# Layer 0's carried-state convolution taps on GpSimd, paced over the input stage and three heads

## What is computed

```python
q, k, v, g_ret, ca, cb, ga, gb = split(rms_norm(x) @ w_in)
o, r_new = retention(q, k, v, r0)          # 4 heads; r0: carried state, 8 sequences x 4 heads x 256 x 512
y_ret = (silu(g_ret) * layer_norm(o)) @ w_ret_out
u = ca * sigmoid(cb)
padded = concatenate([c0, u])              # c0: the last 30 rows of u, carried, for each sample sequence
z = depthwise_conv(padded, conv_w) + conv_b   # 31 taps a channel
x = x + rms_norm((sigmoid(ga) * y_ret + sigmoid(gb) * conv_branch(z)) @ w_o)
x = x + rms_norm(swiglu_ffn(rms_norm(x)))
```

## Time and profile before

| what | value |
| --- | --- |
| median of three executions | 1622.85 us (1619.75 to 1623.2) |
| the profiled execution, its own time | 1627.17 us |
| its span, first to last instruction | 1625.4 us |
| TensorE busy | 1559.7 us, 96% of the span |
| VectorE busy | 1133.8 us, 70% |
| ScalarE busy | 666.1 us, 41% |
| GpSimd busy | 285.8 us, 18% |
| DMA | 275.69 MB, 170 GB/s on average |
| mean granted TensorE clock | 0.989 of full speed |

### The profile page before, as it was taken

The page is one execution under the profiler, slowest core; times in us unless marked ns, Lnnn a source line. Parts: engine busy times, 40 slices in busy tenths (PEclk is TensorE's granted clock), DMA queues, the critical chain, the costliest instruction groups (busy, mean ns, idle before and its releaser), DMA issues.

```text
span 1625.4 us, 28225 instructions
## 1 busy us (share of the span) xinstructions
PE 1559.7 (96%) x10008; PEld 1433.0 (88%) x10008; DVE 1133.8 (70%) x1684; ACT 666.1 (41%) x973; POOL 285.8 (18%) x257
## 2 busy tenths in 40 slices
PE   6988999999999999999989999999999999999997
PEld 5987878786899999999979979687779998999997
DVE  6999887887767577654456988779786675555544
ACT  4323434353455353433343335253445544444433
POOL 6971100001110019910000400001020100000000
PEclk8999999999999999999999999999999999999999
DMA  6444846556344424444435555647364442444443
GB/s 258 143 170 143 292 149 241 194 209 238 124 143 149 171 92 155 153 144 156 156 116 165 199 185 219 220 170 281 136 219 156 149 137 79 160 151 143 154 156 114
DMA packets 64562, 275.69 MB, mean 170 GB/s; under 512 B 7232, under 2 KB 7232, under 8 KB 55232
## 3 DMA queue, kind: packets, MB, share of 16 engines
q1 hardware_dynamic: 52560, 192.17, 34.7%
q0 software_dynamic: 11888, 82.04, 14.0%
HBM read 230.30 MB, written 43.89 MB: 169 GB/s over the span
## 4 chain that ended last, share of the span: by engine, by line
PE 77%; DVE 10%; issue 6%; DMA 4%; ACT 2%; DVEq 0%; POOL 0%; ACTq 0%
PE bank L414 22%; PE bank L416 21%; PE bank L415 21%; DMA rs_out<-state 3%; DVE wlo L1032 2%; DVE acc L1067 2%; PE bank L551 2%; DMA state<-r_in 2%; PE bank L448 1%; PE bank L586 1%; PE bank L568 1%; DVE state L1098 1%; PE bank L534 1%; PE bank L503 1%; DVE x L1336 1%
## 5 line engine op out<-in xcount | busy, mean ns | idle before, releaser
L414 PE MATMUL bank<-hhi,whi 128*128 128x320 f32 x2016 | 656.7, 326 | 11.8 <-DVE wlo L1032 9.2
L1032 DVE TENSOR_TENSOR wlo<-wring,whi 128x1024 fp32r<-128x1024 f32 x363 | 475.0, 1312 | 257.0 <-ACT whi L769 203.0
L416 PE MATMUL bank<-hhi,wlo 128*128 128x320 f32 x2016 | 624.8, 310 | 0.0
L415 PE MATMUL bank<-hlo,whi 128*128 128x320 f32 x2016 | 624.5, 310 | 0.0
L414 PEld LDWEIGHTS bank<-hhi,whi 128*128 128x128 f32 x2016 | 380.1, 189 | 73.1 <-issue 58.3
L415 PEld LDWEIGHTS bank<-hlo,whi 128*128 128x128 f32 x2016 | 380.7, 189 | 6.5 <-issue 3.8
L416 PEld LDWEIGHTS bank<-hhi,wlo 128*128 128x128 f32 x2016 | 380.1, 189 | 0.0
L769 ACT ACTIVATE whi<-wring 128x1024 fp32r<-128x1024 f32 x264 | 277.5, 1055 | 236.9 <-PE bank L416 236.5
L1067 DVE SCALAR_TENSOR_TENSOR acc<-up,par,acc 128x256 f32<-128x256 f32 x480 | 230.0, 544 | 0.0
L795 ACT ACTIVATE whi<-wring 128x1024 fp32r<-128x1024 f32 x96 | 101.4, 1056 | 99.6 <-PE bank L416 99.6
L799 ACT ACTIVATE sig<-bank 128x320 f32<-128x320 f32 x92 | 40.3, 438 | 209.0 <-PE bank L416 195.5
(11 more groups left out here) (155 smaller groups left out, 2012.2 us busy)
## 6 DMA issues: line engine op xcount, KB each, us to landing
wring<-w SPq DMA_DIRECT2D x364, 512.0 KB, 3.3
state<-r_in POOLq DMA_DIRECT2D x32, 1024.0 KB, 7.0
rs_out<-state POOLq DMA_DIRECT2D x32, 1024.0 KB, 5.4
rp_out<-pst POOLq DMA_DIRECT2D x8, 512.0 KB, 7.6
us<-c_in POOLq DMA_DIRECT2D x2, 1216.0 KB, 5.8
cs_out<-us POOLq DMA_DIRECT2D x2, 1216.0 KB, 8.2
cp_out<-up POOLq DMA_DIRECT2D x2, 1144.0 KB, 4.6
con<-consts POOLq DMA_DIRECT2D x1, 1420.0 KB, 9.7
```

What stands on the lines that cost most here:

```text
L414: pe.matmul(bank[g][:, 0:T], whi[j][:, k, :], hi, start=start and k == 0, stop=False)
L415: pe.matmul(bank[g][:, 0:T], whi[j][:, k, :], lo, start=False, stop=False)
L416: mm = pe.matmul(bank[g][:, 0:T], wlo[j][:, k, :], hi, start=False, stop=stop and k == n - 1)
L1032: return dve.tensor_tensor(dst, value, hi.bitcast(F32), ALU.subtract)
```

## The change

The carried taps of layer 0 are split up. Taps 0 to 3 start as before. Taps 4 to 17 each wait for `unit_done` to reach 2k - 6, so that they run one for every two units, the last of them behind unit 28, the end of head 0. The other twelve, taps 18 to 29, go into GpSimd's work on heads 0 and 1: one behind each of `store(0)`, `store(1)`, `rp_out`, `store(2)`, `store(3)` and the last load. The bias and the save `cs_out` follow behind head 1, and the 8 newest taps are put between the stores and loads of head 2: three behind `load_after(1)`, two behind `rp_out`, one behind `store(2)`, two behind `store(3)`. `cp_out` is issued behind tap 17. Layer 1's order stays, and so do the other engines' programs.

```diff
@@ past_taps becomes past_tap and past_bias; layer0_taps and new_tap are new
-            def past_taps(l, past, ptap, bias, weights):
+            def past_tap(l, past, ptap, weights, k):
...
+                n = min(DS, PAD - k)
...
+                pool.tensor_tensor(window(ptap if k else past, 0, n), window(us, k, n), tap, ALU.mult).then_inc(sample_conv_step, 1)
+                if k:
+                    pool.wait_ge(sample_conv_step, l * SAMPLE_OPS + 2 * k)
+                    pool.tensor_tensor(window(past, 0, n), window(past, 0, n), window(ptap, 0, n), ALU.add).then_inc(sample_conv_step, 1)
+
+            def past_bias(l, past, bias):
...
+            first_taps = iter(range(PAD))
+
+            def layer0_taps(n, unit=None):
+
+                for k in itertools.islice(first_taps, n):
+                    if unit is not None and k > 3:
+
+                        pool.wait_ge(unit_done, 2 * k - 6)
+                    past_tap(0, past0, stap, par[:, G_CW:NPAR], k)
+
+            def new_tap(l, i):
...
@@ in head(l, hd, last)
-                for q in range(2):
-                    store(q)
-                    load_after(q)
+                spread = l == 0 and hd < 2
+                newest = iter(range(DS) if l == 0 and hd == 2 else ())
+                store(0)
+                if spread:
+                    layer0_taps(1)
+                load_after(0)
+                store(1)
+                if spread:
+                    layer0_taps(1)
+                load_after(1)
+                if l == 0 and hd == 2:
+
+                    pool.wait_ge(u_saved, 32)
+                    for i in itertools.islice(newest, 3):
+                        new_tap(l, i)
 
                 pool.wait_ge(act_aux, H * AUX_ACT + 7)
                 pool.dma_start(rp_out[H], pst[:, :, :]).then_inc(pst_stored, 16)
+                if spread:
+                    layer0_taps(1)
+                for i in itertools.islice(newest, 2):
+                    new_tap(l, i)
                 store(2)
+                if spread:
+                    layer0_taps(1)
+                for i in itertools.islice(newest, 1):
+                    new_tap(l, i)
                 store(3)
+                for i in newest:
+                    new_tap(l, i)
                 if not last:
+                    if spread:
+                        layer0_taps(1)
                     load_after(2)
                     load_after(3)
+                if spread:
+                    layer0_taps(1)
@@ in the layer loop
-                    past_taps(0, past0, stap, par[:, G_CB:G_CW], par[:, G_CW:NPAR])
+                    layer0_taps(PAD - 12, U_CIN)
 
                 pool.wait_ge(u_ready, l * 16 + 16)
                 pool.dma_start(cp_out[l], up[:, :, :]).then_inc(u_saved, 16)
+                if l == 0:
+                    for hd in range(2):
+                        head(l, hd, False)
+                    past_bias(0, past0, par[:, G_CB:G_CW])
                 pool.wait_ge(sample_conv_step, l * SAMPLE_OPS + PAST_OPS)
                 pool.dma_start(cs_out[l], us[:, :, :, :]).then_inc(u_saved, 16)
-
-                pool.wait_ge(u_saved, l * 32 + 32)
-                new_taps(l)
-                for hd in range(HEADS - 1):
-                    head(l, hd, False)
+                if l > 0:
+
+                    pool.wait_ge(u_saved, l * 32 + 32)
+                    for i in range(DS):
+                        new_tap(l, i)
+                    for hd in range(2):
+                        head(l, hd, False)
+                head(l, 2, False)
                 conv_pair_sum(l, 1)
                 head(l, HEADS - 1, True)
```

More of the change, by code:

```diff
@@ L385, in _ @@
                     pool.wait_ge(ffn_step, l * (2 * FT) + 2 * FFN_FIRST)
-                    past_taps(l + 1, past, ptap, cw[:, 0:KT], cw[:, KT:KT * (1 + TAPS)])
+                    for k in range(PAD):
+                        past_tap(l + 1, past, ptap, cw[:, KT:KT * (1 + TAPS)], k)
+                    past_bias(l + 1, past, cw[:, 0:KT])
                 pool.wait_ge(unit_done, l * UNITS + UNITS)
```

30 lines of the change are left out of this document (11 added, 19 removed).

## The result

The changed kernel took 1632.35 us (median of six executions, 1630.91 to 1634.6), the kernel before 1624.28 us (six, the three known ones among them, 1619.75 to 1626.23). The ratio is 1.0047, 95% interval 1.0036 to 1.0058: slower by 0.5%, where 1610.5 us were predicted, with a range of 1603 to 1617. The profiled execution of the changed kernel took 1631.73 us with a span of 1629.9; that of before took 1627.17, above its own median, so the two traces are only 4.6 us apart where the medians are 8.1 apart.

What follows compares the result with a forecast made beforehand. TensorE, busy 96%, was taken to bound the kernel, with gains only where it waits or runs at half clock. 1627.2 - 19.3 + 7 = 1614.9 us for the profiled execution, median 1610.5, range 1603 to 1617.

Steps and rivals of the forecast that it cites:

- Heads 1 to 3, where late steps of heads 0 to 2 run: Taps moved there delay the chain of late steps between TensorE and VectorE: 7 us lost in all, bounds 0 and 12.
- First units: Start of layer 0: fourth hlo free of GpSimd, five groups end at 33.0 instead of 38.19 us; gain 5.2.
- Input stage: Fourth unit to last up: VectorE's pair with one tap, about 6.4 us, fits under TensorE's 7.04; gain 11.9.
- Head 0: Layer 0's head 0, with taps 11 to 17: VectorE full, layer 1's value taken; gain 2.2 us, bounds 0 and 3.1.
- Head 1: Taps 18 to 23 between stores and loads, each priced by the slack at its place: 3.9 us lost.
- Taps 22 and 23 fall on work with slack: In head 1's stretch, the last two of its six carried taps were given no cost.
- Price of a tap: Each GpSimd instruction costs VectorE about 0.83 us where it always has such work, a tap of two 1.65.
- Head 2: Taps 24 to 29, shorter at 384 down to 64 elements, cost about half: 1.8 us lost.
- Newest taps: Eight taps in head 3's stretch, sixteen instructions, the two largest where there is slack: 1.5 us lost.
- DMAs: Loads and stores issued on GpSimd between taps: no delay, or 0.5 us behind tap 18; counted as costing nothing.
- The slower rival: GpSimd's queue delays carried states, 8 us for each of three heads, 24 us lost, time 1627.5; chance 0.06.
- the likeliest case: Whole kernel: both the early gain and the head costs occur, 1607 to 1614 us; chance 0.60.

Runs made afterwards that it cites:

- run 10: Change with heads' taps all behind last loads, plus no input-stage tap before the fourth unit, then one a unit for twelve, then one per two: 1610.04 us, 0.9902 of before.
- run 3: Against the change: taps 0 to 17 back to back without the pacing, heads as in the change; 1633.62 us, 1.0050 of before.
- run 6: Against the change: heads' taps all moved behind the last loads and taps 0 to 17 unpaced; 1616.22 us, 0.9941 of before.
- run 5: Against run 2: in heads 0 and 1 the tap behind store(0) moved behind the last load; 1617.87 us, 0.9953 of before.
- run 4: Against the change: the twelve carried taps in heads 0 and 1 each replaced by four memsets, which read nothing; 1619.19 us, 0.9940 of before.
- run 2: Against the change: only the eight newest taps moved, in one block behind head 2's last load; 1623.85 us, 0.9981 of before.
- run 11: Against run 10: four carried taps behind head 0's last load and eight behind head 1's, instead of six and six; 1609.6 us, 0.9889 of before.
- run 12: Against run 11: the eighteen taps of input stage and head 0 at one per one and a half units; 1604.97 us, 0.9856 of before.

## Why the prediction was wrong

It was right on what bounds the kernel and on the size of the gain in the input stage, and wrong on the step "Heads 1 to 3, where late steps of heads 0 to 2 run", which put the loss at 7 us with a bound of 12. It was 21.4. That is 14.4 of the 16.8 us between the 1614.9 forecast for the profiled execution and its 1631.7; the rest is gain that did not come in the first units and head 0.

- **First units**, predicted 5.2, measured 3.9 (TensorE's fourth unit at 34.30, "near 33"). The clock of the stretch stayed at 0.81, with 6.8 us at the half level around the wait of 3.06 us for `hlo`. The prediction took it that those waits go, but the four taps that stayed, 16.0 to 25.5 us, meet the first three `hlo`, and run 10 shows that without them both wait and half clock go.
- **Input stage**, predicted 11.9, measured 57.91 - 46.11 = 11.8. `up` comes every 7.04 us, the last at 80.34, no wait for `wlo`. A paced tap cost VectorE 1.2 us, not 1.65, with no effect on the time. The number is right, but the reason given, that one tap a pair fits under TensorE's 7.04 us, is not what it hangs on: without the pace VectorE needs about 9.6 us a pair for as long as the taps run, and the stage takes 46.1 us all the same (run 3). Eighteen taps in place of thirty are over, at 70.8 us, before VectorE's lead over TensorE is used up. By runs 3 and 6 the pace is worth some 3 us, all in the first units.
- **Head 0**, predicted 2.2, measured 0.3. VectorE was full, as the prediction says; seven taps took its room. Together 16.0 by the last `sg` (17.0 by the mark of unit 28) instead of 19.3.
- **Head 1**, predicted 3.9, measured 9.6. The first wait went as foretold ("from 0.77 to about 2.5", 2.80). Then three sub-steps failed. The delays were priced one by one, each from its own slack, but VectorE's list is one chain: what it loses behind `store(0)` uses up the slack at the next place (run 5). "Taps 22 and 23 fall on work with slack" missed that the slack belongs to `oT` and `sqo`: four and six of VectorE's taps ahead of `oT` took 3.81 and 4.61 us instead of 1.67 and 2.46, and TensorE waited 2.08 us. And no price was put on the half clock behind a longer wait, 3.4 us here, though the page's clock and the earlier trace rows had shown what it costs in the first units.
- **Price of a tap.** The 1.7 us came from a mean over the input stage of before. Behind `store(0)` a tap of 2.41 us cost 2.03, where VectorE was doing nothing but two-input work. The Trainium skill's page SBUF — State Buffer, section "SBUF: two separate sides", has the loser blocked for the whole instruction, for a VectorE instruction with two SBUF inputs only against a GpSimd instruction that reads SBUF. This case's runs agree with both: 2.03 of 2.41 us, and nothing beside memsets (run 4). The prediction's split into two-input work that suffers and PSUM work that does not leaves out a third kind: the two `TENSOR_SCALAR` at 333.11 us, which read one tensor, took 1.15 and 1.40 us beside the newest taps, against 0.41 for each in layer 1.
- **Head 2**, predicted 1.8 (shorter taps), measured 2.0.
- **Newest taps**, predicted 1.5 since "the two largest lie where there is slack", measured 9.8 (run 2). Sixteen instructions stand from 314.5 to 335.4 us with a single wait among them, 2.70 us. In that time VectorE's taps and `wlo` all run long, up to `oT` at 339.11, and the waits of 2.27 and 3.24 with their half clock are the sum. This dense block left no slack around it, whatever lay beside its largest piece.
- **DMAs**, predicted nothing, measured nothing up to head 3 (with the tap done, the load at 148.00 still waited 1.85 us for its store to land). The slower rival, GpSimd's queue delaying carried states by 24 us, didn't happen: up to 352 us no query waits for its load, and the wait of 1.78 in before went; one of 1.15 at 404.34 is all there is. The kernel became slower by the mechanism of the likeliest case, at three times its size, and not by the one that the prediction named for slower.

With the measured terms the sum closes: 1627.2 - 17.0 + 21.4 = 1631.6, the profiled execution's own 1631.7. It closes this well only because two steps further on cancel: 3.1 us more between unit 64 and the start of layer 1, of which that wait of 1.15 is one, and 2.9 less within layer 1. They weren't taken apart, and are no larger than the scatter there.

## What to carry to other kernels

Price work on GpSimd by what VectorE does beside it at that moment, and put it where VectorE's next result is not waited for; between the stores and loads of this hand-over chain there was least room, however idle GpSimd looked. A stage whose helper runs some units ahead can take a burst of such work for nothing, as long as the burst ends before the lead does. Along an engine's fixed list delays add up until an idle gap, so the slack of one place can be spent once. And count behind each new TensorE wait of some 2 us the half clock that may follow it: here it cost nearly as much as the waits themselves, though the same wait does not always bring it.

## What the runs showed of the hardware that wasn't expected

- In the changed kernel's heads, stretches at half clock of 3.4 or 6.8 us stand at or behind five of the six waits of 1.5 to 3.2 us (the one of 2.08 has none), and behind one of the three waits of 1.12. Over before, half their length makes 10.2 us, beside 11.4 us of waits.
- Four memsets of GpSimd for each tap, in the place of the tap, cost VectorE's two-input taps nothing (478 ns, as in before and in layer 1 without GpSimd); a multiply and an add cost 2.03 us of their 2.41.
- Keeping GpSimd quiet for the first 28 us brought the fourth unit 10.2 us forward against before (runs 10 to 12), nearly as much as the whole input stage gained. Not all of it is VectorE's time: the granted clock rose from 0.77 to 1.00.
- Eighteen GpSimd taps in a row beside the input stage made VectorE's `up` come 9.6 us apart instead of 7.04 and cost TensorE nothing there (46.1 us either way), since VectorE worked three units ahead (run 3).
